# A hybrid decoder step on one core: the first gate product moved ahead of the parameter and state transposes

## The reference, cut to what matters

```python
def conv_module(x, past, w_pw1, b_pw1, w_dw, b_dw, g_cn, b_cn, w_pw2, b_pw2):
    h = x @ w_pw1 + b_pw1
    u = h[..., :D_MODEL] * jax.nn.sigmoid(h[..., D_MODEL:])
    ext = jnp.concatenate([past.astype(u.dtype), u], axis=1)
    conv = lax.conv_general_dilated(
        ext, w_dw[:, None, :].astype(ext.dtype), window_strides=(1,), padding='VALID',
        dimension_numbers=('NWC', 'WIO', 'NWC'), feature_group_count=D_MODEL) + b_dw
    z = layer_norm(conv, g_cn, b_cn)
    z = z * jax.nn.sigmoid(z)
    return z @ w_pw2 + b_pw2, ext[:, -CONV_STATE:]
```

## Time and profile before

| what | value |
|---|---|
| runs of the kernel before, us | 1176.74, 1177.2, 1186.55 |
| their median, us | 1177.2 |
| the profiled execution, us | 1187.07 |
| its span in the trace, us | 1185.4 |
| mean granted clock of PE, share of full speed | 0.903 |
| PE busy, us (share of the span) | 987.3 (83%) |
| DVE busy, us | 409.8 (35%) |
| ACT busy, us | 174.3 (15%) |
| POOL busy, us | 104.2 (9%) |

### The profile page before, as it was taken

The page is one execution under the profiler, slowest core; times in us unless marked ns, Lnnn a source line. Parts: engine busy times, 40 slices in busy tenths (PEclk is TensorE's granted clock), DMA queues, the critical chain, the costliest instruction groups (busy, mean ns, idle before and its releaser), DMA issues.

```text
span 1185.4 us, 14389 instructions
## 1 busy us (share of the span) xinstructions
PE 987.3 (83%) x4730; PEld 481.7 (41%) x4731; DVE 409.8 (35%) x896; ACT 174.3 (15%) x333; POOL 104.2 (9%) x196
## 2 busy tenths in 40 slices
PE   3989988779989999949989784579788899998993
PEld 3656535323323333326646543245443233333331
DVE  2545445322233323361134422121431432233236
ACT  1000123111001110111122322111211011111000
POOL 2050000101000000023000002200020000000000
PEclk7989988799989999979899897789869899999998
DMA  7584532799969999938030102309269369999981
GB/s 209 148 261 124 170 124 93 242 384 363 372 222 352 379 381 383 375 94 284 14 142 1 41 23 67 89 19 393 92 206 343 147 238 376 376 378 372 384 307 45
DMA packets 131606, 267.19 MB, mean 225 GB/s; under 512 B 7370, under 2 KB 39142, under 8 KB 131539
## 3 DMA queue, kind: packets, MB, share of 16 engines
q1 hardware_dynamic: 121184, 237.75, 56.6%
q10 hardware_dynamic: 4979, 16.15, 3.9%
q0 software_dynamic: 5392, 12.60, 3.9%
HBM read 260.04 MB, written 7.15 MB: 225 GB/s over the span
## 4 chain that ended last, share of the span: by engine, by line
PE 68%; DVE 11%; DMA 8%; SPq 5%; issue 4%; ACT 3%; ACTq 0%; POOL 0%; DVEq 0%
PE bank L944 11%; PE bank L936 10%; PE wide L936 8%; PE bank L976 4%; PE bank L874 4%; PE bank L762 3%; PE wide L874 2%; PE wide L762 2%; PE bank L1687 2%; DMA w<-in_e_w 2%; PE bank L778 2%; DMA w<-in_state_conv 2%; PE bank L1588 2%; DMA dbuf<-in_a_w_pw 2%; PE bank L979 1%
## 5 line engine op out<-in xcount | busy, mean ns | idle before, releaser
L944 PE MATMUL bank<-w,dbuf 128*64 128x512 f32 x512 | 133.7, 669 | 18.2 <-DVE dbuf L1344 18.2
L936 PE MATMUL bank<-w,dbuf 128*64 128x512 f32 x512 | 119.2, 619 | 7.2 <-DMA w<-in_e_w 3.2
L936 PE MATMUL wide<-w,dbuf 128*64 128x512 f32 x512 | 113.4, 595 | 0.9 <-DMA w<-in_e_w 0.9
L1349 DVE COPY dbuf<-bank 64x512 f32<-64x512 f32 x64 | 44.1, 689 | 136.6 <-PE bank L944 136.2
L976 PE MATMUL bank<-dbuf,ukT 128*128 128x512 f32 (+1 forms) x144 | 79.4, 655 | 12.7 <-DVE dbuf L1359 5.9
L944 PEld LDWEIGHTS bank<-w,dbuf 128*64 128x64 f32 x512 | 44.7, 151 | 83.4 <-issue 83.2
L936 PEld LDWEIGHTS bank<-w,dbuf 128*64 128x64 f32 x512 | 42.5, 143 | 79.8 <-issue 78.1
L1687 PE MATMUL bank<-ident,w 128*128 128x128 f32 (+1 forms) x192 | 33.6, 330 | 35.3 <-DMA w<-in_cache_ckv 27.2
L936 PEld LDWEIGHTS wide<-w,dbuf 128*64 128x64 f32 x512 | 35.4, 137 | 66.0 <-issue 63.9
L530 POOL COPY idx_col<-idx 64x1 int32 (+1 forms) x32 | 5.7, 178 | 598.2 <-PE bank L923 426.4
L517 POOL DMA_DIRECT2D w<-in_cache_kpe x64 | 34.3, 536 | 267.8 <-PE bank L1742 165.0
(11 more groups left out here) (338 smaller groups left out, 1267.4 us busy)
## 6 DMA issues: line engine op xcount, KB each, us to landing
w<-in_e_w SPq DMA_DIRECT2D x90, 2048.0 KB, 18.6
dbuf<-in_a_w_pw SPq DMA_DIRECT2D x16, 512.0 KB, 6.1
w<-in_cache_ckv SPq DMA_DIRECT2D x64, 128.0 KB, 2.2
w<-u_rows SPq DMA_DIRECT2D x32, 142.0 KB, 2.9
dbuf<-in_a_w_pw ACTq DMA_DIRECT2D x1, 4096.0 KB, 16.0
dbuf<-in_e_w SPq DMA_DIRECT2D x2, 2048.0 KB, 16.4
dbuf<-in_b_w_o SPq DMA_DIRECT2D x1, 4096.0 KB, 12.9
x_tok<-in_e_w SPq DMA_DIRECT2D x2, 1536.0 KB, 17.3
```

The source lines that it names most:

```text
L936: last = nc.tensor.matmul(bank[n * C:(n + 1) * C], x[:, k], w[n][k], start=(k == 0), stop=(k == KD - 1))
L944: last = nc.tensor.matmul(bank[n * C:(n + 1) * C], h[:, k], w[k][:, n * 512:(n + 1) * 512], start=(k == 0), stop=(k == 3))
L1349: last = V.tensor_copy(y_pair[s * C:(s + 1) * C, h * 512:(h + 1) * 512], B[4 + s][h * C:(h + 1) * C, :])
```

## The change

Three things move, and no instruction is added or taken away.

- PE: the definitions of `gated`, `conv`, `pivot` and `add_channels` go ahead of the turns, and with them the call of `gated(0)`, behind the wait for all six copies of `xT`. The parameter and state turns follow it. `gated(0)` no longer waits for `glu_done`; `gated(1)` waits for 1 (the parameter copy, which frees bank 2), and later ones for j + 1 as before.
- ACT: the two state loads are issued after the copies of `xT`, and not ahead of the table load.
- POOL: a wait for `h_done`, the end of `gated(0)`, stands ahead of its nine loads, so the two stores come later as well.

```diff
             nc.gpsimd.memset(zeros, 0.0).then_inc(pad_set, 1)
+            pool.wait_ge(h_done, 1)
             pool.dma_start(rw[:], a["r_w"].rearrange("(k p) e -> p k e", p=P)).then_inc(ld_misc, 16)
...
             act.dma_start(dw_rows[0:CW], a["a_w_dw"][0]).then_inc(ld_vec, 16)
+            act.wait_ge(ones_set, 1)
+            nc.scalar.activation(spare2[:, 1:2], spare2[:, 0:1], ACT.Sigmoid)
+            copy_xT(act, 0)
             for h in range(2):
                 act.dma_start(state[0:4 * CS, h],
                               a["state_conv"][0, 4 * h:4 * h + 4].rearrange("b s d -> (b s) d")).then_inc(ld_state, 16)
-            act.wait_ge(ones_set, 1)
-            nc.scalar.activation(spare2[:, 1:2], spare2[:, 0:1], ACT.Sigmoid)
-            copy_xT(act, 0)
...
+            def gated(j):
+
+                s = j % 2
+                pe.wait_ge(pw1_ready[s], (j // 2 + 1) * 32)
+                if j:
+                    pe.wait_ge(glu_done, j + (j > 1))
+                if j >= 2:
+                    pe.wait_ge(glu_p, j - 1)
...
+            pe.wait_ge(xT_copied, 6)
+            gated(0)
             pe.wait_ge(ld_vec, 16 * (len(VECS) + 1))
...
-            pe.wait_ge(xT_copied, 6)
             pe.wait_ge(ones_set, 1)
-
-            def gated(j):
-
-                s = j % 2
-                pe.wait_ge(pw1_ready[s], (j // 2 + 1) * 32)
-                pe.wait_ge(glu_done, j + 1)
...
-            gated(0)
             gated(1)
             gated(2)
```

More of the change, by code:

```diff
@@ L734, in pe_program @@
                 turn_tile(pe, 0, 0, i)
[L736 to L749, removed]
-            pe.wait_ge(xT_copied, 6)
-            pe.wait_ge(ones_set, 1)
             def gated(j):
@@ L796, in add_channels @@
                     .then_inc(sq_used, 1)
+            pe.wait_ge(xT_copied, 6)
             gated(0)
+            pe.wait_ge(ld_vec, 16 * (len(VECS) + 1))
+            nc.tensor.transpose(B[2][:, 0:NVEC], vec_rows[0:NVEC], ident[0:NVEC, 0:NVEC])
+            for k in range(KD):
+                last = nc.tensor.transpose(B[2][:, 64 + k * CW:64 + (k + 1) * CW], dw_rows[0:CW, k * P:(k + 1) * P],
+                                           ident[0:CW, 0:CW])
+            last.then_inc(par_turned, 1)
+            pe.wait_ge(ld_state, 32)
+            for h in range(2):
+                for q in range(2):
+                    for k in range(4):
+                        last = nc.tensor.transpose(B[4 + 2 * h + q][:, k * 4 * CS:(k + 1) * 4 * CS],
+                                                   state[0:4 * CS, h, (4 * q + k) * P:(4 * q + k + 1) * P],
+                                                   ident[0:4 * CS, 0:4 * CS])
+                    last.then_inc(par_turned, 1)
+            pe.wait_ge(ones_set, 1)
             gated(1)
```

## The result

| what | before | after |
|---|---|---|
| median of 20 runs each, us | 1179.55 | 1184.78 |
| lowest and highest, us | 1174.26 to 1186.55 | 1178.82 to 1189.93 |
| profiled execution, us | 1187.07 | 1180.25 |
| its span, us | 1185.4 | 1178.6 |
| mean granted clock of PE | 0.903 | 0.921 |

The ratio of the runs is 1.0042, with a 95% interval from 1.0022 to 1.0062: the changed kernel is slower by 5.0 us (0.0042 x 1179.55). I had forecast 1176.9, within 0.3 us of no change, with a range up to 1184; the median lies above that range. In percent it is inside the 1% that I gave a chance of 0.89, but the interval excludes no change.

What follows compares the result with a forecast made beforehand. The fifth gate block's weight load was taken as the bound: gains of 8.0 us after the first gate product, 5.3 after the second, 2.1 at the third's start, -0.3 at the fifth; from median 1177.2 to 1176.9, range 1171 to 1184.

Steps and rivals of the forecast that it cites:

- The bound: Early chain of waits: a saving reaches the end only if w(4), the fifth gate block's load (19.73 us wait), lands earlier.
- When w(0) lands: First gate block's weights: landing at 18.0 instead of 26.1 us, with GpSimd's and the state's transfers out of the way.
- g(0): First gate product on PE: takes 11.7 us at the low clock and ends at 29.7 instead of 37.70.
- The turns behind it: Parameter turns on PE after the first gate product: 0.9 us, so DVE starts at 30.6 instead of 22.05.
- DVE waits for nothing up to glu(0): Sign in the profile after: DVE runs without a gap from about 30.6 to its first gate multiplication at about 41.
- SP: SP's queue: third block's weights w(2) issued at 38.4, landing 5.8 us later at 44.2; PE idles 3.2 us.
- The sign I named: Profile after: SP's load of the third gate block's weights is released by DVE and not by PE.
- Rival 2: DVE's late start passes to later loads and bounces; w(0) at 21 gives +3.0 us, 1180.2; chance 0.15.
- Rival 1: w(0) lands at 15.1 and DVE's train is short enough; g(4), the fifth gate product, 3.7 us earlier: 1173.5; chance 0.28.
- Rival 4: GpSimd's postponed transfers collide with w(2) and two bounces: +3.5 us, 1180.4; chance 0.10.
- Rival 3: w(0) stays at 26.1 because GpSimd's loads never held it; everything behind is 8 us late: 1185; chance 0.05.

Runs made afterwards that it cites:

- later loads alone: Kernel before with only GpSimd's loads held until the first gate product ends and the state loads after the copies of xT: 1180.51 us, ratio 1.0004.
- SP's wait later: Changed kernel with SP's wait for the state copies moved behind its load of the third gate block's weights: 1180.43 us, ratio 1.0014.
- pw2 issued later: The combined version with ScalarE's load of pw2 issued after block 4 instead of block 2: 1173.34 us, ratio 0.9931.
- PE's order alone: Kernel before with only PE's move of the first gate product; state and GpSimd loads stay early: 1190.28 us, ratio 1.0091.
- taps split: Changed kernel with the load of 31 tap rows issued as two loads of 16 and 15 rows: 1175.92 us, ratio 0.9975.
- without the state: Changed kernel with ScalarE's two state loads held until the first gate product ends, taps in one load: 1177.99 us in a single run.
- GpSimd silent: Changed kernel with GpSimd's wait raised from h_done 1 to 5, so its loads and stores follow the fifth gate product: 1185.06 us, ratio 1.0049.
- parameters first: Changed kernel with the 9 parameter turns put back ahead of the first gate product, state turns behind it: 1185.64 us, ratio 1.0050.
- the two versions with later loads: Later loads alone, 1180.51 us, and the same with GpSimd's wait raised from h_done 1 to 5, 1174.65 us, ratio 0.9956.
- combined version: Changed kernel, taps in two loads, parameter turns first, glu(0) before state copies, SP's wait later, GpSimd's wait at h_done 5: 1168.47 us, ratio 0.9907.

## Why the prediction was wrong

**The bound: right for this change.** An early saving counted only through the load of w(4): g(4) waits for it in ten of the twelve versions. It did not hold in all. In the later loads alone PE waits 5.85 us ahead of conv(1) and not at all ahead of g(4); in SP's wait later 3.86 us ahead of conv(1) and only 0.69 ahead of g(4); with pw2 issued later the wait is ahead of g(6).

**When w(0) lands: this step failed.** I took 18.0 and measured 21.9. The step subtracted the mean shares of GpSimd's and ScalarE's queues over 16 engines (7.1 and 3.9 us) from the old landing. Moving GpSimd's and the state's loads together was worth 5.4 us (27.3 with PE's order alone), less than the 7.1 that I took for GpSimd's alone. The mean share was the wrong measure: the second half of w(0) waited for the taps and the state, as both experiments on them show (13.1 with the taps split, 16.9 without the state), on one engine if my reading holds. I had the rule in front of me (124 KB that took until 20.69), wrote that w(0) still meets taps and state there, and then kept "near 19", a value from means. The old row that should have decided was that lateness of the taps: if a 124 KB load issued at 2.96 is late at 20.7, a load that has to pass the same place may be late too. Split, w(0) came at 13.1, below my 15.1 for both queues' shares gone.

**g(0).** 11.51 us measured, 11.7 taken: right. End 33.53 instead of 29.7, all from w(0).

**The turns behind it.** 0.83 us (33.53 to 34.36) against 0.9. DVE started at 34.36 instead of 30.6. The train was as I had it in its order and without a gap, which the sign "DVE waits for nothing up to glu(0)" shows, and a little longer: the tap copies took 4.26 us in place of the 3.75 they took before. State copies ended at 42.7 (38.4), glu(0) began at 45.01 (40.8).

**SP.** The sign I named came: the load of w(2) was released by DVE, not by PE. w(2) needed 6.7 us from issue to landing (42.72 to 49.39), 5.8 taken; with GpSimd silent it was 5.9. PE waited 4.70 us, 3.2 taken, and g(2) ran at the lower pace, 11.47 us, the later of the two ends I gave.

**Rival 2 is what happened.** "It decides from a g(0) that ends after about 30": g(0) ended at 33.5, 3.5 us beyond, and g(4) is 5.4 late. For w(0) at 21 it had +3.0; w(0) at 21.9 makes that +3.9; the tap copies' 0.5 and w(2)'s 0.9 would bring it to 5.3, a sum that no run took apart. The last two are what GpSimd cost here: with it silent they were gone (3.77 and 5.9 us). I gave it 0.15 with "the taps and the state keep their place ahead of the end of w(0)" as evidence. That evidence was right, and deserved more than the mean shares.

**Rival 1** (w(0) early) is the version with taps split: its 3.7 us sooner was measured as 3.9 at g(4). That is in part luck: w(0) came 2.0 us sooner than it had it (13.1 for 15.1), and g(0) took 10.4 us for 11.7. **Rival 4** (the postponed transfers collide) costs about 1 us at most in the changed kernel and some 7.4 us at g(4) with parameters first, where SP's transfers come in time. Between the two versions with later loads it shows 2.6 us at g(4)'s start and nothing at its end. I had missed that whether it bites depends on rival 2. **Rival 3** did not come.

The range: its upper end of 1184 lay 0.8 below the median. It counted from 1177.2, the median of three runs; over 20 runs the same kernel has 1179.55, so of the 7.9 us by which I missed 2.35 were in the base and 5.5 in the change (5.2 between the medians, where I had -0.3).

## What to carry to other kernels

A mean share per queue did not give the landing time of a load (18.0 taken, 21.9 measured): look in the same stretch for a transfer that is late for its size and has an odd first dimension, and try it split (13.1). When an engine's long work is put ahead of short work that another engine waits for, follow the short work: the 0.8 us of parameter turns behind an 11.5 us product moved DVE's whole train. And a transfer that is postponed costs nothing only while those it may meet are late themselves; an isolating run can show next to nothing for a part that costs 7 us once the neighbour is repaired.

## What the runs showed of the hardware that I had not expected

**The clock's column and the pace disagree.** From 22 to 27 us the changed kernel's row has a granted clock of 1.00, the upper of the two levels, yet g(0) took 11.51 us, as long as the product that the earlier trace rows have after a stretch of low clock. The stretch (columns as in the earlier trace rows):

```profile
22.00:27.00 5.00, 4.99 (x10) 3.23 (x11) 0.00 (x0) 0.00 (x0) 0.00 (x0) 1.00 0.26 79
```

The matmuls of L747 in it by form, and those from 28 on (ns min/median/max):

```profile
L747 PE MATMUL bank<-xT,dbuf x10: 657/741/872, 22.0 to 26.9; 128*128 128x320 f32 x10
...
L747 PE MATMUL bank<-xT,dbuf x20: 432/432/433, 27.7 to 32.8; 128*128 128x320 f32 x20
```

Ten matmuls in 5 us at first, twenty in 5.4 us later; the count in a stretch says more than the column. PE had been idle for 11.66 us before. In g(2) of the same kernel, behind 4.70 us of waiting, the column does show the lower level, from 50 to 54:

```profile
50.00:54.00 4.00, 4.00 (x9) 2.50 (x8) 3.93 (x5) 0.00 (x0) 0.00 (x0) 0.50 0.71 180
```

**DVE and GpSimd's issues.** The Trainium skill, SBUF — State Buffer, in the box on DVE blocking DMA, has GpSimd locked out of writing its descriptors by some DVE copies. The trace of this form of copy does not show it: here GpSimd's 11 issues from 33.84 to 40.55 took 6.7 us beside 16 f32 copies of DVE, the same as from 1.68 to 8.36 with DVE idle. It was DVE that slowed: those copies took 4.26 us, and 3.77 with GpSimd silent (row below, of the version with GpSimd behind g(4)). All fourteen profiles agree: 4.26 to 4.28 us in the four where GpSimd issues beside them, 3.72 to 3.77 in the ten where it doesn't. Why was not tried.

```profile
36.08 3.77 DVE L1082 COPY dbuf<-dw_T 32x64 f32<-32x64 f32 x16
```

**A 1 MB load beside a 4 MB one.** In the version with pw2 later, the two 512 KB halves of w(4) landed 5.3 us after their issue (median), before pw2 was issued. In the combined version, beside pw2, they took 13.5 and 20.0 us, and pw2 itself 16.5: the halves, issued within 0.5 us of it, landed 3.0 us ahead of pw2 and 3.9 us behind it, though pw2 is eight times the size of one. Beside pw2 and GpSimd's loads, w(6)'s took 16.6 and 26.1 us, and pw2 23.5.
